# Row pitch of the normalised activations in SBUF: 1048 bytes instead of 1024

## The chip, the cores and the metric

The kernel runs on one core of one Trainium2 chip. Its time is the device time of one execution in microseconds; the kernel before has a median of 1569.7 us over 3 runs (1568.94 to 1570.23).

## The reference, cut to what matters

Two layers, each a feed-forward block, a token mixer and a second feed-forward block, over 256 tokens of width 1024:

```
for l in range(DEPTH):                      # 2
    h = modulate(rms_norm(x, norm_g[l, 0]), sh1, sc1)
    x = x + 0.5 * g1 * swiglu(h, w_ff_in[l, 0], w_ff_out[l, 0])    # 1024 -> 2 x 2816 -> 1024
    h = modulate(rms_norm(x, norm_g[l, 1]), sh2, sc2)
    x = x + g2 * token_mix(h, w_in[l], ..., w_branch[l], w_gate[l], b_gate[l], w_out[l])
    h = modulate(rms_norm(x, norm_g[l, 2]), sh3, sc3)
    x = x + 0.5 * g3 * swiglu(h, w_ff_in[l, 1], w_ff_out[l, 1])
```

`swiglu` is two products with a gate between; `token_mix` projects h with `w_in` (6416 columns) and `w_gate` (3072 columns), runs attention, a recurrence and gated linear attention on the projections, multiplies the three results with `w_branch`, gates and sums them, and multiplies with `w_out`. All of it is float32.

## The kernel before

The activations are kept transposed: the feature is the partition, and a token is a column. A tile of 1024 features by 256 tokens is 8 chunks of 128 features, `[128 partitions, 8, 256]`. A float32 product is made of three in the `fp32r` format: every operand is split into a high part and a low part, and each product is high x high + high x low + low x high. The normalised activations are `h_hi` and `h_lo` (lines 124, 1066 and 1557), and later, for the output product, the merged branches (lines 1356, 1358 and 1894). Weights arrive in slabs of 128 x 2048 float32 in `raw`; ScalarE writes their high part `w_hi` (line 1020), VectorE their low part `w_lo` (line 1509). Both have three slots of 8192 bytes per partition, and a chunk in them starts at a multiple of 1024 bytes.

TensorE takes the slabs in a fixed order that is written out in the program. Every matmul is a weight load (the stationary operand, 128 columns) and a stream of the moving operand over it; none of the loads is used twice. The forms are:

- Line 498, `slab_tile`, called by `product` (line 502): the weights are stationary, and 256 columns of a chunk of activations move, 3 matmuls for each of 8 chunks and each of 2 halves of the slab, 48 per slab. With `(h_hi, h_lo)` it makes the projections and the gates. With `(y_hi, y_lo)` it makes the branches; these two are views of `xm_hi` and `xm_lo`, whose chunks are 258 columns, or 1032 bytes, apart. Lines 522, 528 and 542 are the same form in another order of loops.
- Line 498 in `out_block`: the second feed-forward product, with two chunks of the hidden activations moving, 48 matmuls per slab. The hidden activations are by turns `hid_hi`, `hid_lo` (1024 bytes apart) and the first two chunks of `y_hi`, `y_lo` (1032 bytes apart), as `j` is even or odd.
- Line 673, `row_products`: the first feed-forward product for j from 1 to 10. Here 128 tokens of a chunk of h are stationary, and 512 weight columns move. A j has two slabs, each with 4 chunks, and two halves m of the tokens: 12 matmuls for each slab and m. For j over 1, `turn` (line 642) transposes on TensorE ahead of each of the first slab's halves.
- Line 893: the value projection of the gated attention; h is stationary again, 256 weight columns move.
- Line 628, `lead`: `xm_hi` and `xm_lo` move, 258 columns.

The pieces of one chunk are read in the order (high, high), (high, low), (low, high), and then comes the next chunk. The tensors lie in SBUF in the order of their allocation: `raw`, `w_hi`, `w_lo`, `rgw`, `xT`, `hf`, `h_hi`, `h_lo`, `xm_hi`, `xm_lo`, `hid_hi`, `hid_lo` and the rest. Every size up to `h_lo` is a multiple of 1024 bytes; `xm_hi` and `xm_lo` have 8256 bytes each.

The line that names the operands of the 512-column form is

```
high, low = [b[:, k, m * P:(m + 1) * P] for b in (h_hi, h_lo)]
```

Of the kernel before, what the change touches and what calls it, by code (L numbers as in the profile page):

```python
# [8 lines left out]
F32R = mybir.dt.float32r  # L9
# [8 lines left out]
T = 256  # L18
C = D // P
# [85 lines left out]
def build(nc, x, c, w_ada, b_ada, norm_g, w_ff_in, w_ff_out, w_in, qk_norm_g, attn_sinks, rel_bias,  # L105
# [3 lines left out]
    with ctx:  # L109
        def sb(name, shape, dt=F32):  # L110
            return ctx.enter_context(nc.sbuf_tensor(name, [P] + shape, dt))
# [9 lines left out]

        xT = sb("xT", [C, T])
        hf = sb("hf", [C, T])
        h_hi, h_lo = sb("h_hi", [C, T], F32R), sb("h_lo", [C, T], F32R)
        xm_hi, xm_lo = sb("xm_hi", [C, T + 2], F32R), sb("xm_lo", [C, T + 2], F32R)
        y_hi, y_lo = xm_hi[:, :, 0:T], xm_lo[:, :, 0:T]
        hid_hi, hid_lo = sb("hid_hi", [2, T], F32R), sb("hid_lo", [2, T], F32R)
# [1847 lines left out]
```

## Time and profile before

| | before |
|---|---|
| median of 3 runs | 1569.7 us (1568.94 to 1570.23) |
| the profiled execution | 1569.56 us, its span 1567.8 us |
| TensorE matmul busy | 1545.6 us (99%), 10831 matmuls |
| VectorE, ScalarE busy | 1136.9 us (73%), 808.8 us (52%) |
| HBM read | 330.23 MB, 212 GB/s over the span |

The span is from the first to the last instruction of the profiled execution; 1.8 us of its time lie around it. Starts in the timelines below are given to 0.01 us, so the mean distance of many matmuls can be read to a fraction of a nanosecond, and that of two neighbours cannot. The duration of one matmul covers its passage through the pipeline; the next one starts long before it ends, so it is the distance between starts that adds up to the span.

### The profile page before, as it was taken

Reading aid. Unit: us, or ns where it says so; the run is one execution under the profiler, and the core shown is the slowest. Engines: PE = TensorE matmul, PEld = TensorE weight load, DVE = VectorE, ACT = ScalarE, POOL = GpSimd, SP = SyncE. Lnnn points to the kernel's source line nnn. Section 1 sums busy time; section 2 is a strip of 40 time slices with the busy share of each in tenths; the row PEclk is TensorE's granted clock in tenths of the full one; section 3 lists DMA queues with packets and bytes.
Section 4 is the critical chain, followed back from the end, with each engine's and each line's share of the span. In section 5 each row is a group of like instructions: output and inputs, shape, how many; then the busy total and the mean of one; then the engine's idle time right before and its main releaser. Section 6 shows DMA issues by size and latency. Waiting matters only on the chain.

```text
span 1567.8 us, 25750 instructions
## 1 busy us (share of the span) xinstructions
PE 1545.6 (99%) x10831; PEld 1421.7 (91%) x10831; DVE 1136.9 (73%) x1573; ACT 808.8 (52%) x1010; POOL 25.2 (2%) x29
## 2 busy tenths in 40 slices
PE   7999999999999999999999999999999999999998
PEld 6988888999999999888898888899999899988887
DVE  4787857898555998967778777779855588986444
ACT  3444436888446336443464444577855544464442
POOL 0000000000100000000000000000001000000000
PEclk8899999999999999999999999999999999999999
DMA  9789845554456986788558884454454599586550
GB/s 339 270 282 271 288 137 162 154 158 134 144 165 206 309 296 211 270 269 293 188 188 287 270 293 157 133 166 149 137 160 139 167 315 324 185 292 191 188 184 32
DMA packets 283987, 333.29 MB, mean 213 GB/s; under 512 B 13084, under 2 KB 235200, under 8 KB 283872
## 3 DMA queue, kind: packets, MB, share of 16 engines
q1 hardware_dynamic: 276112, 327.40, 63.8%
q10 hardware_dynamic: 7760, 4.26, 1.2%
q8 instruction: 85, 1.39, 0.4%
q14 instruction: 30, 0.25, 0.0%
HBM read 330.23 MB, written 1.38 MB: 212 GB/s over the span
## 4 chain that ended last, share of the span: by engine, by line
PE 84%; DVE 10%; ACT 3%; issue 1%; DMA 0%; SPq 0%; DVEq 0%; ACTq 0%
PE ps L498 45%; PE ps L673 27%; DVE w_lo L1509 4%; PE ps L893 3%; ACT w_hi L1020 1%; DVE hf L1552 1%; DVE scratch L1406 1%; DVE h_lo L1557 1%; PE ps L642 1%; PE ps L560 1%; PE ps L808 1%; DVE xT L1572 1%; ACT xm_hi L1046 1%; PE ps L754 1%; PE ps L561 1%
## 5 line engine op out<-in xcount | busy, mean ns | idle before, releaser
L1509 DVE TENSOR_TENSOR w_lo<-raw,w_hi 128x2048 fp32r<-128x2048 f32 x237 | 541.9, 2288 | 254.6 <-ACT w_hi L1020 254.6
L1020 ACT ACTIVATE w_hi<-raw 128x2048 fp32r<-128x2048 f32 x237 | 452.4, 1913 | 293.5 <-PE ps L498 209.7
L498 PE MATMUL ps<-h_hi,w_hi 128*128 128x256 f32 x1104 | 317.4, 288 | 1.7 <-DVE w_lo L1509 1.6
L498 PE MATMUL ps<-h_lo,w_hi 128*128 128x256 f32 x1104 | 312.2, 283 | 0.0
L498 PE MATMUL ps<-h_hi,w_lo 128*128 128x256 f32 x1104 | 312.2, 283 | 0.0
L673 PE MATMUL ps<-w_hi,h_hi 128*128 128x512 f32 x640 | 256.6, 401 | 0.6 <-DVE w_lo L1509 0.5
L673 PE MATMUL ps<-w_lo,h_hi 128*128 128x512 f32 x640 | 249.8, 390 | 0.0
L673 PE MATMUL ps<-w_hi,h_lo 128*128 128x512 f32 x640 | 243.4, 391 | 0.0
L498 PEld LDWEIGHTS ps<-h_hi,w_hi 128*128 128x128 f32 x1104 | 211.4, 192 | 9.8 <-issue 7.1
L498 PEld LDWEIGHTS ps<-h_lo,w_hi 128*128 128x128 f32 x1104 | 211.6, 192 | 0.5 <-issue 0.5
L498 PEld LDWEIGHTS ps<-h_hi,w_lo 128*128 128x128 f32 x1104 | 211.5, 192 | 0.0
L498 PE MATMUL ps<-xm_hi,w_hi 128*128 128x256 f32 x704 | 199.0, 283 | 0.0
L498 PE MATMUL ps<-xm_hi,w_lo 128*128 128x256 f32 x704 | 197.7, 281 | 0.0
L498 PE MATMUL ps<-xm_lo,w_hi 128*128 128x256 f32 x704 | 197.3, 280 | 0.0
L1406 DVE SCALAR_TENSOR_TENSOR scratch<-eyr,cond,scratch 128x512 f32<-128x512 f32 x240 | 180.2, 751 | 7.3
L673 PEld LDWEIGHTS ps<-w_hi,h_lo 128*128 128x128 f32 x640 | 120.2, 188 | 25.5
L673 PEld LDWEIGHTS ps<-w_hi,h_hi 128*128 128x128 f32 x640 | 120.3, 188 | 24.2 <-DVE w_lo L1509 1.9
L673 PEld LDWEIGHTS ps<-w_lo,h_hi 128*128 128x128 f32 x640 | 120.5, 188 | 22.6
L498 PEld LDWEIGHTS ps<-xm_hi,w_hi 128*128 128x128 f32 x704 | 132.8, 189 | 0.8
L498 PEld LDWEIGHTS ps<-xm_lo,w_hi 128*128 128x128 f32 x704 | 132.8, 189 | 0.8
L498 PEld LDWEIGHTS ps<-xm_hi,w_lo 128*128 128x128 f32 x704 | 132.7, 188 | 0.0
L498 PE MATMUL ps<-hid_hi,w_lo 128*128 128x256 f32 x384 | 109.1, 284 | 0.0
(282 smaller groups left out, 2230.6 us busy)
## 6 DMA issues: line engine op xcount, KB each, us to landing
raw<-in_w_ff_in_dram SPq DMA_DIRECT2D x176, 512.0 KB, 5.2
eyr<-in_w_ada_dram SPq DMA_DIRECT2D x144, 512.0 KB, 7.0
raw<-in_w_in_dram SPq DMA_DIRECT2D x100, 512.0 KB, 4.7
raw<-in_w_ff_out_dram SPq DMA_DIRECT2D x88, 512.0 KB, 4.4
raw<-in_w_gate_dram SPq DMA_DIRECT2D x48, 512.0 KB, 4.6
raw<-in_w_branch_dram SPq DMA_DIRECT2D x48, 512.0 KB, 4.6
raw<-in_w_out_dram SPq DMA_DIRECT2D x16, 512.0 KB, 4.9
rgw<-in_rg_w_dram ACTq DMA_DIRECT2D x16, 128.0 KB, 2.3
```

Source lines behind the costliest of these rows:

```text
L498: last = mm(outs, a, b[:, cc, :], start=clear and cc == 0 and q == 0, stop=cc == n - 1 and q == 2, skip_group_check=True)
L560: mm(to, ada_raw(2 * b + 1)[:, cc, cols], cond[:, 4 + cc:5 + cc], start=cc == 0, stop=False)
L561: last = mm(to, acc[:, cols], ones[:, 0:1], start=not direct, stop=True)
L642: last = nc.tensor.transpose(ps[:, 6, c * T + m * P:c * T + (m + 1) * P], t512b[:, (2 * m + c) * P:(2 * m + c + 1) * P], ident[:, :])
L673: last = mm(ps[:, bank, :], (high, high, low)[q], w[(0, 1, 0)[q]], start=k == 0 and q == 0, stop=k == C - 1 and q == 2, skip_group_check=True)
L754: last = nc.tensor.transpose(ps[:, 4 + hh, b * P:(b + 1) * P], pr[:, hh, b * P:(b + 1) * P], ident[:, :])
L808: last = mm(ps[:, 2 - g, t * T:(t + 1) * T], rgw[:, g, t, :], xc[:, t, :], start=True, stop=True)
L893: last = mm(ps[:, 1, m * T:(m + 1) * T], a, b, start=cc == 0 and q == 0, stop=cc == C - 1 and q == 2)
L1020: f(w_hi[:, p % SPLIT, :], raw[:, p % RAW, :], ACT.Copy).then_inc(hi_ready, 1)
L1046: f(xm_hi[:, cc, 0:T], xT[:, cc, :], ACT.Copy, scale=ma[:, cc:cc + 1]).then_inc(xhi_ready, 1)
L1406: ins = stt(acc, w[:, cc, :], by, acc, ALU.mult, ALU.add)
L1509: tt(w_lo[:, p % SPLIT, :], raw[:, p % RAW, :], w_hi[:, p % SPLIT, :].bitcast(F32), ALU.subtract).then_inc(lo_ready, 1)
```

## The change

Each of `h_hi` and `h_lo` is allocated with 262 columns in a chunk instead of 256, and is used through a view of the first 256. Chunks are then 262 x 4 = 1048 bytes apart. Nothing reads or writes the six columns behind each chunk, and no instruction is added or removed.

```
-        h_hi, h_lo = sb("h_hi", [C, T], F32R), sb("h_lo", [C, T], F32R)
+        h_hi, h_lo = (sb(n, [C, T + 6], F32R)[:, :, 0:T] for n in ("h_hi", "h_lo"))
```

Each of the two tensors grows by 8 x 24 = 192 bytes per partition, so `h_lo` starts 192 bytes later and everything behind it 384 bytes later.

## Rows read from the trace of the kernel before

**Rows 1.** The page: busy time by engine, granted clock in 40 slices.
```profile
PE 1545.6 (99%) x10831; PEld 1421.7 (91%) x10831; DVE 1136.9 (73%) x1573; ACT 808.8 (52%) x1010; POOL 25.2 (2%) x29
...
PEclk8899999999999999999999999999999999999999
```

**Rows 2.** Waits of PE: engine, line, waited for: us, times, longest.
```profile
PE ps L560 <- DMA eyr<-in_w_ada_dram: 7.2, 1, 7.2
PE ps L615 <- ACT hf L1044: 3.5, 7, 0.9
...
PE ps L498 <- DVE w_lo L1509: 1.6, 2, 0.8
```

**Rows 3.** Groups by line and shape: busy us, mean ns, idle before.
```profile
L498 PE MATMUL ps<-h_hi,w_hi 128*128 128x256 f32 x1104 | 317.4, 288 | 1.7 <-DVE w_lo L1509 1.6
...
L673 PE MATMUL ps<-w_hi,h_hi 128*128 128x512 f32 x640 | 256.6, 401 | 0.6 <-DVE w_lo L1509 0.5
...
L893 PE MATMUL ps<-w_hi,h_hi 128*128 128x256 f32 x128 | 37.0, 289 | 0.0
...
L542 PE MATMUL ps<-h_hi,w_hi 128*128 128x256 f32 x64 | 18.9, 295 | 0.7 <-DVE h_lo L1894 0.7
...
L522 PE MATMUL ps<-h_hi,w_hi 128*128 128x256 f32 x16 | 5.4, 353 | 0.0
```

**Rows 4.** Timeline of PE, one product of h: start us, us.
```profile
416.83 0.28 PE L498 MATMUL ps<-h_hi,w_hi 128*128 128x256 f32 x1
...
422.47 0.28 PE L498 MATMUL ps<-h_hi,w_lo 128*128 128x256 f32 x1
```

**Rows 5.** Timeline of PE, one product of y, 8 chunks.
```profile
524.52 0.28 PE L498 MATMUL ps<-xm_hi,w_hi 128*128 128x256 f32 x1
...
530.11 0.28 PE L498 MATMUL ps<-xm_hi,w_lo 128*128 128x256 f32 x1
```

**Rows 6.** Timeline of PE, two second feed-forward products, hid and y.
```profile
71.31 0.28 PE L498 MATMUL ps<-hid_hi,w_hi 128*128 128x256 f32 x1
...
76.95 0.29 PE L498 MATMUL ps<-hid_hi,w_lo 128*128 128x256 f32 x1
...
88.48 0.28 PE L498 MATMUL ps<-xm_hi,w_hi 128*128 128x256 f32 x1
...
94.01 0.29 PE L498 MATMUL ps<-xm_hi,w_lo 128*128 128x256 f32 x1
```

**Rows 7.** Timeline of PE, 512-column form, the last 24 of 36.
```profile
83.04 0.39 PE L673 MATMUL ps<-w_hi,h_hi 128*128 128x512 f32 x1
...
88.25 0.39 PE L673 MATMUL ps<-w_hi,h_lo 128*128 128x512 f32 x1
```

**Rows 8.** Timeline of PE, the 12 of that form behind two transposes.
```profile
197.00 0.48 PE L673 MATMUL ps<-w_hi,h_hi 128*128 128x512 f32 x1
197.31 0.39 PE L673 MATMUL ps<-w_lo,h_hi 128*128 128x512 f32 x1
...
198.93 0.39 PE L673 MATMUL ps<-w_hi,h_lo 128*128 128x512 f32 x1
...
199.61 0.39 PE L673 MATMUL ps<-w_hi,h_lo 128*128 128x512 f32 x1
```

**Rows 9.** Two stretches (products of h and of y): us, PE, PEld, DVE, ACT, POOL, clock.
```profile
416.84:422.48 5.64, 5.64 (x50) 5.64 (x48) 2.29 (x1) 5.43 (x4) 0.00 (x0) 1.00 0.00 0
524.52:530.11 5.59, 5.59 (x50) 5.59 (x49) 4.64 (x5) 2.65 (x3) 0.00 (x0) 1.00 1.06 383
```

**Rows 10.** Groups by line and shape, ScalarE and VectorE: writers of h, two chunks at once.
```profile
L1356 ACT ACTIVATE h_hi<-hf 128x512 fp32r<-128x512 f32 x6 | 3.8, 626 | 8.8 <-DVE hf L1831 8.8
L1894 DVE TENSOR_TENSOR h_lo<-hf,h_hi 128x512 fp32r<-128x512 f32 x8 | 5.5, 687 | 1.4 <-ACT h_hi L1358 1.4
```

## The prediction

> **What bounds the kernel now.** I read the page's busy times first, then TensorE's waits, and then, since they leave one engine to explain, its timeline. TensorE is busy for 99% of the span and VectorE for 73% [rows 1]. TensorE's waits for others are 16.9 us, of which 7.2 us are the first load of data; the wait for split weights, the supply that could take over as the bound, comes to 1.6 us in two waits [rows 2]. So the time is the sum of the distances between the starts of 10831 matmuls, and a nanosecond on one of them is a nanosecond of the time. The granted clock is full but for the first two slices [rows 1] and 1.00 in the stretches that I measure [rows 9], the 2.4 GHz level. There 256 columns take 106.7 ns and 512 columns 213.3 ns; what a matmul takes beyond that is what the change can touch.
>
> Take the distances from the timeline. A product of h has 48 matmuls, 47 distances in 422.47 - 416.83 = 5.64 us: 120.0 ns each [rows 4]. A product of y is the same instruction over the same columns with chunks 1032 bytes apart, and takes 530.11 - 524.52 = 5.59 us: 118.9 ns each [rows 5]. The second feed-forward product gives a cleaner pair: with `hid` (pitch 1024) 5.64 us, 120.0 ns; with y (pitch 1032) 5.53 us, 117.7 ns [rows 6]. The last two stand in the same place of the same loop. So the pitch of the chunks matters, and 1024 is the worse of the two tried here in the form that moves activations.
>
> The 512-column form has two levels. Well away from an interruption, 24 starts lie 5.21 us apart, 226.5 ns each [rows 7]. Behind the transposes, the first distance is 310 ns, then come seven over 198.93 - 197.31 = 1.62 us, 231.4 ns each, then three at 226.7 ns [rows 8]. The addresses are as regular at the beginning of these 12 as at the end. My reading: the stream of the moving operand and the load of the next stationary one disturb each other by their relative position, and over equal addresses they drift into one position and stay there. In the 256-column form that settled position (120.0) is worse than the places passed elsewhere; in the 512-column form the settled one (226.7) is better than those passed on the way (231.4).
>
> **The change part by part.** No instruction goes or comes. What changes is where chunks start: h moves 24 bytes per chunk relative to the weights, whose chunks stay at multiples of 1024. That acts on three sets.
>
> (a) h moving over 256 columns: 3 x 1104 at line 498, 3 x 64 at line 542, 48 at lines 522 and 528 (of which one group is shown), 3552 in all [rows 3]. Today they take 119.8 on average, by my count over the settled 120.0 and the few steps after each interruption. The bounds are 120.0 (the pitch does nothing here) and 117.7, the best product of y: 0 to -2.1 x 3552 = -7.5 us. I take 118.5, between the y product of 8 chunks, which is the same loop [rows 5], and that of two [rows 6], since a step three times that of y should leave a settled position more surely: -1.3 x 3552 = -4.6 us.
>
> (b) line 893, weights moving over 256 columns and h stationary: 384 matmuls [rows 3]. No row shows a stationary operand off the 1024 grid. Bounds by the same rows, -0.8 us and, if it goes by what the unsettled 512-column form does (4.7 ns over its settled level), +1.8 us; I take the same -1.3 ns as in (a), since its column count is that form's: -0.5 us.
>
> (c) line 673: 1920 matmuls [rows 3], of which 80 are the first of a group after another form and keep their long distance, 1840 distances. Today's mean over them is 227.7: 226.7 when settled, and some 24 ns of extra per group behind transposes (five to seven distances at 231.4), 72 such groups, 1.7 us in all or 1.0 ns on the mean. After the change the stationary address moves at every third matmul, faster than the seven or so distances that settling takes [rows 8]. So it should hardly settle. The lower bound is to carry over what y leaves beyond the clock's columns, 117.7 - 106.7 = 11.0 ns, hence 224.3: -3.4 x 1840 = -6.3 us. The upper one takes the 4.7 ns that the seven unsettled distances lie over the settled level and, since they are a mean of few, half as much again: 226.7 + 7.0 = 233.7, +6.0 x 1840 = +11.0 us. I take 230, nearer to the unsettled row than to the settled: +2.3 x 1840 = +4.2 us.
>
> At nothing: the later start of the tensors behind h, by 192 or 384 bytes, which are multiples of 64. `hid` already lies 128 bytes off the grid by the sizes ahead of it, and its product takes the 120.0 of h [rows 4, 6]. Writers that cover two chunks in one instruction now step over a gap, 14 of the shown form [rows 10] of 0.6 to 0.7 us each. If a gap cost 50 ns, the few on the way to the output product would make 0.3 us. The faster 256-column slab asks for weights some 0.06 us sooner; VectorE is busy 4.64 of 5.59 us and 2.29 of 5.64 in two such stretches [rows 9], so the cover stays.
>
> Sum: -4.6 - 0.5 + 4.2 = -0.9 us. Against the profiled execution's 1569.56 that is 1568.7; that execution stands 0.14 under the median of 1569.7, so 1568.8.
>
> The Trainium skill, "TensorE: Matmul & The Clock Gate" (Part 2), says that TensorE has two independent SBUF read ports and that loading the next weights takes no read bandwidth from the running matmul. By that rule the sum would be 0. The pair of rows 6 speaks against it, since only the moving operand's addresses differ there.
>
> **The rivals.** First, both forms gain: loss of the settled position pays wherever it happens, and 231.4 is an effect of the transposes and not of being unsettled. For it: the y products, the only ones with uneven addresses, are all lower. Against: the seven slow distances go on for 1.6 us after the last transpose [rows 8]. With 224.9 in (c): -2.8 x 1840 = -5.2, and -5.1 from (a) and (b), -10.3 us: 1559.4.
>
> Second, slower: the 512-column form pays for every uneven load. The place is line 673; the price is anything over 227.7 ns per distance, and it decides from 227.7 + 5.1/1840 us = 230.5 ns on, where it has eaten what (a) and (b) bring. At 233.7 it costs 11.0 us, in sum +5.9: 1575.6. For it: distances above 231 do occur behind transposes, and in a 512-column stream with one load per 213 ns the load is not what limits, so that any disturbance falls on the stream. Against: seven distances are a thin base for a mean. The Trainium skill's "SBUF — State Buffer" (SBUF: two separate sides, on cachelines) adds a reason: lines are 16 bytes and each new line costs, and odd chunks would begin 8 bytes into one. This trace doesn't bear it out for the moving operand, as y has the same 8 bytes and is lower [rows 5]; for a stationary one no row here shows it.
>
> Third, the pitch of h does nothing: the difference between h and y is not its pitch but, say, where these tensors lie. Rows 6 against it: one y product is equally short early in the run, with two chunks only. 1569.7.
>
> **How the numbers follow.** What tells from no change is about 0.2%, 3.1 us. The forecast, cancelling to within 3 us, 0.35; both gain 0.30; slower 0.25; nothing 0.10. The forecast's case gives 0.08 to faster and 0.04 to slower, the slower rival leaves 0.05 within 0.2%: faster 0.38, same 0.38, slower 0.24. The bounds together reach from -7.5 - 0.8 - 6.3 = -14.6 to +1.8 + 11.0 = +12.8. Leaving out some 2 in 10 at ends that need all terms at their worst, the range is 1558 to 1577; the forecast's own is 1565.7 to 1571.9.
>
> **What would show it.** The product of h at about 417 us: 5.57 us over its 47 distances instead of 5.64 (118.5 ns). Twenty-four distances of the 512-column form away from transposes: 230 ns where 226.5 stands now, and no longer two levels within one group of 12. The y and `hid` products unchanged at 5.59 and 5.64 us. Counts of instructions and waits of TensorE unchanged. The prediction is wrong in (a) if the product of h stays at 120.0, in (c) if line 673 falls below 226.5, and in its whole reading if y or `hid` move as well, since then the place of a tensor counts and not its pitch.

## The result: 8 us slower

The changed kernel takes 1577.62 us (median of 5, 1574.33 to 1577.86) against 1569.58 us for the one before in the same runs (1566.25 to 1570.23). The ratio is 1.0051, with a 95% interval of 1.0037 to 1.0066. In both kernels one execution of the five is some 3 us shorter than the others, so medians are compared. The profiled execution has a span of 1575.5 us, 7.7 more than before. The instructions of TensorE are the same, and it waits for others no more than it did. The page's first line and TensorE's waits (us in total, times, longest) after the change:

```profile
PE 1554.0 (99%) x10831; PEld 1422.1 (90%) x10831; DVE 1137.5 (72%) x1573; ACT 809.2 (51%) x1010; POOL 25.2 (2%) x29
```

```profile
PE ps L560 <- DMA eyr<-in_w_ada_dram: 6.9, 1, 6.9
PE ps L615 <- ACT hf L1044: 3.4, 7, 1.0
...
PE ps L498 <- DVE w_lo L1509: 1.8, 3, 0.8
```

PE is 8.4 us busier, and the three waits shown stand within 0.3 us of [rows 2]. So the loss is in the matmuls. The timeline of PE after the change (start us, us), in the order of rows 6, 7, 8, 4 and 5:

```profile
71.11 0.28 PE L498 MATMUL ps<-hid_hi,w_hi 128*128 128x256 f32 x1
...
76.73 0.29 PE L498 MATMUL ps<-hid_hi,w_lo 128*128 128x256 f32 x1
...
82.88 0.40 PE L673 MATMUL ps<-w_hi,h_hi 128*128 128x512 f32 x1
...
88.23 0.40 PE L673 MATMUL ps<-w_hi,h_lo 128*128 128x512 f32 x1
88.47 0.28 PE L498 MATMUL ps<-xm_hi,w_hi 128*128 128x256 f32 x1
...
94.11 0.29 PE L498 MATMUL ps<-xm_hi,w_lo 128*128 128x256 f32 x1
...
202.12 0.40 PE L673 MATMUL ps<-w_lo,h_hi 128*128 128x512 f32 x1
...
203.75 0.39 PE L673 MATMUL ps<-w_hi,h_lo 128*128 128x512 f32 x1
...
204.45 0.40 PE L673 MATMUL ps<-w_hi,h_lo 128*128 128x512 f32 x1
...
418.56 0.28 PE L498 MATMUL ps<-h_hi,w_hi 128*128 128x256 f32 x1
...
424.14 0.29 PE L498 MATMUL ps<-h_hi,w_lo 128*128 128x256 f32 x1
...
525.83 0.29 PE L498 MATMUL ps<-xm_hi,w_hi 128*128 128x256 f32 x1
...
531.46 0.28 PE L498 MATMUL ps<-xm_hi,w_lo 128*128 128x256 f32 x1
```

Read them as distances. The 512-column form away from transposes: (88.23 - 82.88)/23 = 232.6 ns, where [rows 7] gave 226.5. Behind the transposes: 1.63/7 = 232.9 and 0.70/3 = 233 ns; the second, lower level of [rows 8] is gone. The product of h: 5.58/47 = 118.7 instead of 120.0 [rows 4]. And two that I had not expected: y over 8 chunks 5.63/47 = 119.8 instead of 118.9 [rows 5], y over two chunks 5.64/47 = 120.0 instead of 117.7 [rows 6], although the change leaves the pitch of y alone.

The mean distance from a matmul of each kind to the next matmul, in ns, counted from each kernel's trace. Interruptions are left out (distances above 130 ns, or above 245 ns in the 512-column form), and the number before the change stands in brackets. The experiments of the next section stand beside them:

| | h moves (3468) | line 893 (374) | 512 columns (1835) | y moves (2078) | hid moves (1142) |
|---|---|---|---|---|---|
| before | 119.8 | 119.9 | 227.9 | 118.4 | 119.7 |
| after | 119.0 | 118.5 | 232.6 | 119.7 | 119.7 |
| e1, places only | 119.8 | 119.9 | 228.2 | 119.1 | 119.8 |
| e2, pitch only | 119.0 | 118.6 | 232.7 | 118.4 | 118.7 |
| e4, mixer only | 119.0 | 118.6 | 227.8 | 118.4 | 119.8 |
| e6, start 32 | 119.7 | 119.9 | 233.1 | 118.3 | 118.7 |
| e7, mixer 0 / 8 | 119.5 | 117.8 | 227.8 | 118.4 | 119.7 |
| e9, mixer 8 / 8 | 118.8 | 116.0 | 227.8 | 118.4 | 119.7 |
| e11, mixer 32 / 32 | 117.0 | 118.3 | 227.9 | 118.4 | 119.7 |
| e12, mixer, hid 192 | 115.3 | 116.1 | 228.1 | 118.3 | 117.7 |

From before to after: +4.7 x 1835 = +8.7 us in the 512-column form, +1.36 x 2078 = +2.8 in y, -0.8 x 3468 = -2.8 in h, -1.4 x 374 = -0.5 at line 893, +8.2 in sum. After the change three distances fewer lie under the limits; summed as they are, the five columns grow by 7.7 us, which is what the span grew by.

### The profile page after: what moved, and what is told of

Its sections match the earlier page's. It is cut to its first block, busy times and chain, and to the rows that moved or that the text cites. A ratio compares the mean times of both kernels' runs of the same rounds, so it can differ in the third digit from the quotient of the medians.

```text
span 1575.5 us, 25750 instructions
## 1 busy us (share of the span) xinstructions
PE 1554.0 (99%) x10831; PEld 1422.1 (90%) x10831; DVE 1137.5 (72%) x1573; ACT 809.2 (51%) x1010; POOL 25.2 (2%) x29
## 4 chain that ended last, share of the span: by engine, by line
PE 86%; DVE 7%; ACT 4%; issue 1%; DMA 0%; SPq 0%; ACTq 0%; DVEq 0%
PE ps L498 44%; PE ps L673 28%; PE ps L893 3%; DVE w_lo L1509 2%; PE ps L628 1%; ACT w_hi L1020 1%; DVE scratch L1406 1%; PE ps L642 1%; PE ps L560 1%; PE ps L808 1%; DVE hf L1552 1%; DVE h_lo L1557 1%; PE ps L754 1%; ACT xm_hi L1046 1%; PE ps L561 1%
## 5 line engine op out<-in xcount | busy, mean ns | idle before, releaser
L498 PE MATMUL ps<-hid_hi,w_hi 128*128 128x256 f32 x384 | 109.3, 285 | 0.3
```

Of the source, the lines that this page charges most:

```text
L498: last = mm(outs, a, b[:, cc, :], start=clear and cc == 0 and q == 0, stop=cc == n - 1 and q == 2, skip_group_check=True)
```

## The experiments

A "place" is where a chunk starts against the start of the weights' chunk, modulo 256 bytes, written high part / low part. The weights' chunks start at multiples of 256 bytes in every run, so only the activations move. By the allocation, h is at 0 / 0 before; in the changed kernel its first chunks are at 0 / 192 and each next one 24 further. xm and y are at 0 / 64 before and at 128 / 192 after, hid at 128 / 128 and at 0 / 0.

**e1: only the places of what lies behind h.**

```
         h_hi, h_lo = sb("h_hi", [C, T], F32R), sb("h_lo", [C, T], F32R)
+        gap = sb("gap", [96])
```

> h keeps its pitch of 1024 bytes; only a gap of 384 bytes stands behind h_lo, so that xm, hid and all behind them start where they do in the changed kernel. Theory A (place counts as well as pitch: the y matmuls of line 498 got longer in the changed kernel, from 118.4 to 119.7 ns on average, because their tensors moved by 384 bytes): y at 119.7 ns, lead (line 628) a little longer, h at 120.0 and the 512-column form at 226.7 settled as before; about +3 us, ratio 1.002. Theory B (y got longer since the matmuls of h around it changed, and place does nothing): all distances as before, ratio 1.000.

1570.7 against 1568.8 us, ratio 1.0015 (1.0006 to 1.0024). In its timeline y over 8 chunks is as long as after the change, 5.63 us, and a product of h stays at 120.0:

```profile
416.67 0.28 PE L499 MATMUL ps<-h_hi,w_hi 128*128 128x256 f32 x1
...
422.31 0.28 PE L499 MATMUL ps<-h_hi,w_lo 128*128 128x256 f32 x1
...
524.54 0.28 PE L499 MATMUL ps<-xm_hi,w_hi 128*128 128x256 f32 x1
...
530.17 0.28 PE L499 MATMUL ps<-xm_hi,w_lo 128*128 128x256 f32 x1
```

So place alone costs, theory A. But over all of y it is 119.1 and not 119.7: half of y's loss appears only with h at pitch 1048 as well. The missing half is the y product of two chunks, 117.8 before, 118.4 here and 120.0 after the change. It stands behind the 512-column form, and its own addresses are the same in e1 and after the change. So what it is entered from seems to matter, which e10 takes up at other places; this one was not entered several ways.

**e2: only the pitch of h, the rest at its old places.**

```
         h_hi, h_lo = (sb(n, [C, T + 6], F32R)[:, :, 0:T] for n in ("h_hi", "h_lo"))
+        mod = sb("mod", [DEPTH, 72])
+        ma, ms = sb("ma", [C]), sb("ms", [C])
...
-        mod = sb("mod", [DEPTH, 72])
-        ma, ms = sb("ma", [C]), sb("ms", [C])
```

> h at pitch 1048 as in the change, but mod, ma and ms (640 bytes) are allocated right behind h_lo, so that xm, hid and the rest start at their old places modulo 1024. Theory A: y returns to 118.4 ns and hid to its old distances, h stays at 119.0, line 893 at 118.5 and the 512-column form at 232.6; about -3 us against the changed kernel, +5 us against the one before, ratio 1.003. Theory B: as the changed kernel, ratio 1.005.

1573.89 against 1568.8 us, ratio 1.0032 (1.002 to 1.0043), as A said. One part of A missed: `hid`, at its old place, fell from 119.7 to 118.7, and again the form ahead of it is what changed. The 512-column form and y over two chunks in its timeline, (85.54 - 80.19)/23 = 232.6 ns and 5.53/47 = 117.7:

```profile
80.19 0.40 PE L673 MATMUL ps<-w_hi,h_hi 128*128 128x512 f32 x1
...
85.54 0.40 PE L673 MATMUL ps<-w_hi,h_lo 128*128 128x512 f32 x1
85.78 0.28 PE L498 MATMUL ps<-xm_hi,w_hi 128*128 128x256 f32 x1
...
91.31 0.29 PE L498 MATMUL ps<-xm_hi,w_lo 128*128 128x256 f32 x1
```

**e3: TensorE alone.** The stretches are written over one buffer of weights and one of activations:

```
for k in range(8):
    at = [b + k * pitch for b in bases]
    ...                                  # three matmuls, as in line 498 or line 673
```

> Only TensorE works, on 36 stretches of 96 matmuls in the two forms, each stretch with its own pitch and start of the activations; the rest of the computation is left out, and no other engine or transfer runs beside it. Theory A (weight load and moving stream of TensorE disturb each other by their relative addresses): the first stretch, 512 columns at pitch 1024, settles at 226.7 ns, pitch 1048 gives 232 to 233; 256 columns at pitch 1024 settle at 120.0, at 1048 lie at 118 to 119.5. If the period of the addresses is 64 bytes, pitch 1088 and 1152 are as 1024. Theory C (the disturbance comes from DMA writes or the other engines' reads and writes of SBUF, only timed by the addresses): all stretches near the clock's columns, 216 and 109 ns, whatever the pitch.

The page of this run has ScalarE at 14.1 us and a DMA share of 0 between the first and the last slice, and the granted clock is 1.00 from 50 to 620 us. Whole stretches of 96 matmuls in its timeline (start us, us): 512 columns at pitch 1048, pitch 1280, pitch 1048 with 0 / 192, start 16, start 32 and start 256; then 256 columns at pitch 1024 start 0, at pitch 1048 with 0 / 192, at pitch 1032 with 0 / 64 (y's place before the change) and 128 / 192 (its place after), and at start 256.

```profile
85.84 22.58 PE L112 MATMUL ps<-w,a 128*128 128x512 f32 x96
...
175.35 22.05 PE L112 MATMUL ps<-w,a 128*128 128x512 f32 x96
...
197.27 22.50 PE L112 MATMUL ps<-w,a 128*128 128x512 f32 x96
...
241.90 22.01 PE L112 MATMUL ps<-w,a 128*128 128x512 f32 x96
...
263.78 22.64 PE L112 MATMUL ps<-w,a 128*128 128x512 f32 x96
...
331.19 22.03 PE L112 MATMUL ps<-w,a 128*128 128x512 f32 x96
...
397.70 11.75 PE L108 MATMUL ps<-a,w 128*128 128x256 f32 x96
...
489.78 11.64 PE L108 MATMUL ps<-a,w 128*128 128x256 f32 x96
...
501.29 11.65 PE L108 MATMUL ps<-a,w 128*128 128x256 f32 x96
...
512.81 11.72 PE L108 MATMUL ps<-a,w 128*128 128x256 f32 x96
...
581.62 11.75 PE L108 MATMUL ps<-a,w 128*128 128x256 f32 x96
```

The settled distances, each the mean of a stretch's last 48, are 226.67 ns for pitch 1280 and starts 16 and 256, 233.33 for start 32, 231.7 to 232.8 for pitch 1048; and 120.00, 118.9, 118.9, 119.7, 120.00 for 256 columns. The two for y are those of its product of 8 chunks in the kernels, 118.9 before and 119.8 after. So the effect is TensorE's own and needs no transfer and no other engine: theory C falls. A shift by 256 bytes is no shift; pitches 1088 and 1152 are not like 1024 (231.7, 231.8), so 64 bytes are not the period, and 128 neither.

**e4: pitch 1048 in the mixer only.** Two views of the same memory:

```
+        h_hi, h_lo = (b[:, :].rearrange("p (c t) -> p c t", c=C)[:, :, 0:T] for b in (b_hi, b_lo))
+        f_hi, f_lo = (b[:, s:s + C * T].rearrange("p (c t) -> p c t", c=C) for b, s in ((b_hi, 0), (b_lo, 16)))
...
-                        high, low = [b[:, k, m * P:(m + 1) * P] for b in (h_hi, h_lo)]
+                        high, low = [b[:, k, m * P:(m + 1) * P] for b in (f_hi, f_lo)]
```

> As e2, but the two feed-forward blocks view the same memory of h with chunks 1024 bytes apart, both parts starting at a multiple of 256 bytes; only the token mixer keeps 1048. This takes the 512-column form out of the change. Theory A (the loss is the 512-column form's, the mixer's products gain): line 673 back at 227.9 ns on average and 226.7 settled, h at 119.0, line 893 at 118.5; about 3 us under the kernel before, ratio 0.998, and 8 us under e2. Theory D (uneven addresses cost by themselves, in the mixer through waits or other work too): not under the kernel before, ratio 1.000 or more.

1566.57 against 1569.1 us, ratio 0.9981 (0.9972 to 0.999), and 7.3 us under e2. Its 512-column form is back at (88.84 - 83.63)/23 = 226.5 ns, and its product of h keeps the gain, 5.58 us:

```profile
83.63 0.39 PE L675 MATMUL ps<-w_hi,h_hi 128*128 128x512 f32 x1
...
88.84 0.39 PE L675 MATMUL ps<-w_hi,h_lo 128*128 128x512 f32 x1
...
416.78 0.28 PE L500 MATMUL ps<-h_hi,w_hi 128*128 128x256 f32 x1
...
422.36 0.29 PE L500 MATMUL ps<-h_hi,w_lo 128*128 128x256 f32 x1
```

This isolates the loss of e2: it is in the form in which h is loaded while 512 weight columns move.

**e5: more starts, TensorE alone.** As e3, with another list of places.

> TensorE alone again, the rest of the computation left out: 32 stretches at pitch 1024 with other starts of the two parts, and four of the form of line 893 (256 weight columns move, activations stationary). Theory A with a period of 256 bytes: for 512 columns no start is better than 0 or 16, the others lie at 230 to 234 ns; for 256 columns moving all starts but 0 lie at 117.5 to 119; line 893's form is 120.0 at start 0 and 118 to 119 elsewhere. If instead only a few starts I happened to try are bad, some of the new ones in the 512-column form come below 226.7, the next lower multiple of 6.67 ns being 220.0.

For 512 columns, starts 144 and 240 and the pairs 0 / 16, 16 / 0 and 0 / 240 settle at 226.67 too, start 192 at 228.9; all others lie from 231.1 to 234.4, none below 226.67. For 256 columns moving the spread is wide: 123.3 at start 4, 120.0 at 24 and 96, 117.2 at 240, 115.6 at 0 / 8. "All starts but 0" was wrong, and so was 118 to 119 for line 893's form, which settles at 115.6 at start 8.

**e6: even pitch, another start.**

```
+        h_hi, h_lo = (b[:, 0:C * T].rearrange("p (c t) -> p c t", c=C) for b in (b_hi, b_lo))
+        f_hi, f_lo = (b[:, 8:8 + C * T].rearrange("p (c t) -> p c t", c=C) for b in (b_hi, b_lo))
```

> Pitch 1024 everywhere; but in the two feed-forward blocks both parts of h start 32 bytes behind a multiple of 256. All other tensors and the mixer's view of h keep their places modulo 1024. Theory A (what counts is where a chunk stands against the weights, modulo 256 bytes; uneven pitch is only one way to leave the good place): the 512-column form at 233.3 ns as in e3's stretch at start 32, 5.4 over today's 227.9, so +10 us, ratio 1.006. Theory E (my forecast's: the settled level is lost only because the chunks are uneven): 226.7 and no change, ratio 1.000.

1576.57 against 1569.02 us, ratio 1.0043 (1.003 to 1.0057). Twenty-four starts of the 512-column form in its timeline, (89.19 - 83.82)/23 = 233.5 ns:

```profile
83.82 0.40 PE L676 MATMUL ps<-w_hi,h_hi 128*128 128x512 f32 x1
...
89.19 0.40 PE L676 MATMUL ps<-w_hi,h_lo 128*128 128x512 f32 x1
```

With perfectly even chunks the form takes 233.1 ns on average, more than in the changed kernel. So the loss needs no unevenness; leaving a good place is enough. The run came out 2.4 us under the expectation, 1.2 us of it since hid fell to 118.7.

**e7: the place that was best alone.** The mixer's `h_lo` starts 8 bytes on: `((b_hi, 0), (b_lo, 2))`.

> Pitch 1024 everywhere, the feed-forward view as before. In the mixer h_hi starts at a multiple of 256 bytes and h_lo 8 bytes behind one. From e5's stretch at 0 / 8: h moving over 256 columns at 115.6 ns instead of 119.8, 3552 matmuls less the 64 of the first block, so -14.6 us; line 893 somewhere from 115.6 to 120, 0 to -1.6 us; in sum 15 us under the kernel before, ratio 0.990. Theory F (a stretch of TensorE alone does not carry over, since waits, transposes and other engines' traffic come between): the gain is under half of that.

1567.65 against 1569.02 us, ratio 0.9994 (0.9985 to 1.0002): 1.4 us instead of 15. A miss, and theory F looked right. But two products of h in its timeline take (522.91 - 517.48)/47 = 115.5 ns and (540.93 - 535.30)/47 = 119.8 ns at the same addresses:

```profile
517.48 0.28 PE L501 MATMUL ps<-h_hi,w_hi 128*128 128x256 f32 x1
...
522.91 0.27 PE L501 MATMUL ps<-h_hi,w_lo 128*128 128x256 f32 x1
...
535.30 0.28 PE L501 MATMUL ps<-h_hi,w_hi 128*128 128x256 f32 x1
...
540.93 0.29 PE L501 MATMUL ps<-h_hi,w_lo 128*128 128x256 f32 x1
```

Cut into pieces of 24 uninterrupted distances, the products of h in e7 have 8 pieces at 115.5 to 115.8 ns, 80 at 119.3 to 120.1, and none between.

**e8: pairs with 8 bytes between, and pitch 1032.** As e5.

> TensorE alone, the rest of the computation left out: line 893's form at 0 / 8, other pairs of starts with the low part 8 bytes on, and pitch 1032 with 18 pairs of starts, to see which place would serve y. If 0 / 8 is good because the parts alternate by 8 bytes, every hi/hi+8 pair is near 115.6 ns; if it is that pair alone, the others are spread over 117 to 123 as in e5.

Other pairs 8 bytes apart lie from 117.8 to 118.9 ns, so 0 / 8 is alone in its 115.6 (and has it at pitch 1280 too, the period of 256 again). At pitch 1032 eighteen pairs spread over 117.5 to 120.3. The pair of y, 0 / 64, was 118.9 in e3, and I left it.

**e9 and e10: does the entry decide?** e9 has 8 / 8 in the mixer; e10 enters 16 places five times each behind a matmul of 64, 96, 130, 164 or 202 columns.

> As e7, but in the mixer both parts of h start 8 bytes behind a multiple of 256, pitch 1024; the feed-forward view starts at 0. Theory A with several cycles per place (in e7 the stream fell into the 120 ns cycle of its place and not the 115.6 one): at 8 / 8 e3 gave 117.5 ns; if that place has one cycle only, h is at 117.5 in all products, 3488 x -2.3 = -8 us, line 893 at 115.5 to 118, -0.7 to -1.7 us: 9 us under the kernel before, ratio 0.994. Theory F (no stretch measured alone carries over): h somewhere in 118.5 to 120, ratio 0.998 or more.

> TensorE alone, the rest of the computation left out: 16 places, each entered five times behind a matmul of another length (64 to 202 columns). If a place can hold several cycles, 0 / 8 shows both 115.6 and about 120 ns for 256 columns, and the entry decides. If each place has one, all five are equal, and e7's 119.5 must come from other engines. The 512-column form at 0 / 0 is 226.7 for all five by either.

e10's timeline, whole stretches of 72 matmuls: 0 / 0 once, the last two at 8 / 8, and the first three at 192 / 192.

```profile
265.51 8.88 PE L108 MATMUL ps<-a,w 128*128 128x256 f32 x72
...
335.53 8.84 PE L108 MATMUL ps<-a,w 128*128 128x256 f32 x72
344.30 8.64 PE L108 MATMUL ps<-a,w 128*128 128x256 f32 x72
...
481.40 8.43 PE L108 MATMUL ps<-a,w 128*128 128x256 f32 x72
489.71 8.42 PE L108 MATMUL ps<-a,w 128*128 128x256 f32 x72
498.02 8.70 PE L108 MATMUL ps<-a,w 128*128 128x256 f32 x72
```

The same addresses hold different cycles. 8 / 8 runs at 120.0 ns after four entries and at 117.5 after one; 0 / 8 at 120.0 after four and at 115.6 after one; 192 / 192 at 113.33 after two and at 117.8 after three; 32 / 32 at 116.7 or 117.8. Others keep to one: 0 / 0 at 120.0, 12 / 12 at 117.5, and all three places tried with 512 columns at 226.67. That explains e7's two levels without other engines, and e9 as well: 1564.55 against 1568.87 us, ratio 0.9973 (0.9963 to 0.9984), half of what one cycle at 117.5 would give, its products of h having 45 pieces of 24 distances at 117.5 to 118.5 ns and 43 at 119.7 to 120.1. Line 893's form kept one distance through all five entries, 115.5 at 8 / 8 and 117.8 at 0 / 8, and the kernels have 116.0 (e9) and 117.8 (e7).

**e11 and e12: places whose worst cycle is good.** e11 puts the mixer's view at 32 / 32; e12 puts it at 192 / 192, with the feed-forward view 64 bytes on, at 0, and hid at 192 / 192 too:

```
+        h_hi, h_lo = (b[:, 0:C * T].rearrange("p (c t) -> p c t", c=C) for b in (b_hi, b_lo))
+        f_hi, f_lo = (b[:, 16:16 + C * T].rearrange("p (c t) -> p c t", c=C) for b in (b_hi, b_lo))
...
+        gap = sb("gap", [16])
         hid_hi, hid_lo = sb("hid_hi", [2, T], F32R), sb("hid_lo", [2, T], F32R)
```

> As e9, but the mixer's h starts 32 bytes behind a multiple of 256. In e10 that place held 116.7 or 117.8 ns and never 120.0, whatever the entry. Theory A with cycles: h between 116.7 and 118.0 in all products, 3488 x -2.1 to -3.1 = -7 to -11 us, line 893 0 to -1.4 us: 7 to 12 us under the kernel before, ratio 0.992 to 0.9955. Theory F (other engines' traffic decides as much as the place): 118.5 or more, ratio 0.997 or more.

> The mixer's h and hid both start 192 bytes behind a multiple of 256, y and lead keep their places, the feed-forward view of h is at 0. In e10 that place held 117.8 or 113.3 ns. Theory A with cycles: h and hid at 117.8 or less, 3488 x -2.0 = -7 us and 1152 x -1.9 = -2 us: at least 9 us under the kernel before, ratio 0.994 or less, and up to 25 us where 113.3 is found. Theory F: ratio 0.997 or more.

e11: 1561.33 against 1568.95 us, ratio 0.9952 (0.994 to 0.9965). e12: 1555.68 us, ratio 0.992 (0.9906 to 0.9933), 13 us under the kernel before and 22 under the changed one. Both lie in the ranges of A with cycles. Two products of h in e12's timeline show both cycles that e10 found, 5.54/47 = 117.9 and 5.33/47 = 113.4 ns:

```profile
412.67 0.28 PE L502 MATMUL ps<-h_hi,w_hi 128*128 128x256 f32 x1
...
418.21 0.28 PE L502 MATMUL ps<-h_hi,w_lo 128*128 128x256 f32 x1
...
531.02 0.28 PE L502 MATMUL ps<-h_hi,w_hi 128*128 128x256 f32 x1
...
536.35 0.28 PE L502 MATMUL ps<-h_hi,w_lo 128*128 128x256 f32 x1
```

The distances gain more than the time does. The five columns of the table sum to 18.4 us less in e12 than before, and the span is 13.6 us shorter. TensorE now waits longer for others: three of its waits (us in total, times, longest), of which the first two were 3.5 and 1.6 us before [rows 2], and the third did not come to 0.5 us before:

```profile
PE ps L619 <- ACT hf L1048: 4.6, 7, 1.6
PE ps L502 <- DVE w_lo L1513: 2.6, 3, 1.1
...
PE ps L801 <- ACT t512a L1228: 2.1, 4, 0.6
```

## Why the prediction was wrong

The direction of both forms was right, and so was that waits and other engines add nothing. Two sizes were not, nor was the later start of the tensors behind h, costed at nothing, and the time fell just outside the range. By the prediction's own last sign its whole reading fell as well, since y moved: what counts is the place of a chunk, and the pitch acts by moving the chunks from place to place.

- Step (c) put the 512-column form at 230 ns, nearer to the unsettled row than to the settled. It measured 232.6 (after) and 232.7 (e2): +8.7 us instead of +4.2. The unsettled 231.4 of [rows 8] was the better guide than anything below it, and still not the level; e3 shows 231.4 to 232.8 for the uneven pitches 1032 to 1056 and 233.3 for an even shift by 32 bytes. The reason given, that uneven chunks prevent settling, isn't needed for the loss: e6 has even chunks and takes 233.1.
- "At nothing: the later start of the tensors behind h" was the step that failed outright. It rested on 64 bytes being as good as none. The period is 256 (e3), 384 is not a multiple of it, and y paid 2.8 us. e1 gives half of that by place alone; the other half comes only with the changed 512-column form ahead of it. `hid` at 128 with the 120.0 of h was no sign that 128 bytes do nothing: the same place has 118.7 in e2 and e6.
- Step (a) took 118.5 ns and got 119.0: -2.8 us instead of -4.6. Its argument, that a step three times that of y leaves the settled position more surely, had no row; e3 has 118.9 for this very place and pitch.
- Step (b), from the same rows, came out at -1.4 ns against -1.3, inside its bounds. That is luck in part: it took the value of (a), which missed, and no row had this form off the 1024 grid.
- The pair of [rows 6] was read as showing pitch alone, but `hid` and y differ in place too, 128 / 128 against 0 / 64. For h and y in [rows 4] and [rows 5] the pitch does make the difference: e3 has 120.0 at 0 / 64 with pitch 1024 and 118.9 with pitch 1032.
- The second rival named the right place and price: line 673, deciding from 230.5 ns. It had 0.25. The third, where tensors lie, had 0.10 and took h's pitch to do nothing; place does count, and e2 shows that h's pitch does too.
- The Trainium skill, "TensorE: Matmul & The Clock Gate" (Part 2), has weight load and moving stream on independent read ports, the load taking no read bandwidth from the running matmul. It says nothing of addresses. The sum of 0 that the prediction read from it is not borne out: with TensorE alone (e3) the distance moves from 226.7 to 233.3 ns by a shift of 32 bytes in the loaded operand. The lines of 16 bytes in the Trainium skill's "SBUF — State Buffer" (SBUF: two separate sides) don't sort the measured starts either: 16 and 32 both start a line and lie at the best and near the worst of the 512-column form (226.7 and 233.3).

What stays open is the mechanism inside. That two read streams meet in parts of SBUF that repeat every 256 bytes would fit, but no run here separates it from another cause with the same period. No run moved the weights either, so it is not shown whether the place counts against the weights' or by itself. Nor do the runs say why 0 is among the best places for the 512-column form and nearly the worst for the 256-column one.

## What to carry to other kernels

When TensorE's own stream bounds a kernel, take the distance between starts, not the duration, and compare it over places of the operands: here a few hundred bytes of padding are worth from +0.5% to -0.8%. The good place differs by form, so an operand that is loaded in one phase and moved in another wants two views, and padding one tensor shifts all behind it: keep their places modulo 256 bytes while testing. Count on a place for its worst cycle only, and enter each one several ways before trusting a stretch measured alone. And expect less than the distances promise once TensorE begins to wait for others, as in e12.

## What the runs showed of the hardware

- With `fp32r` operands and a weight load for each matmul, the distance between matmuls depends on the start of the activations' chunk modulo 256 bytes (the weights' chunks at multiples of 256): 226.7 to 234.4 ns for 512 columns (e3, e5), 113.3 to 123.3 ns for 256 (e5, e10), at a granted clock of 1.00, the 2.4 GHz level.
- A stream falls into a cycle and stays in it; 226.67, 233.33, 120.00 and 113.33 ns are all multiples of 6.67 ns, others (117.8, 231.1) are not. The same addresses can hold two cycles up to 4.5 ns apart (117.8 and 113.3 at 192 / 192).
